# Memory values of the cross attention as three products of split parts, and what is moved for them

## What is computed

```python
def memory_cross_attention(h, mem_n, w_q, w_kv, w_o):
    b, s, _ = h.shape
    m = mem_n.shape[1]
    q = (h @ w_q).reshape(b, s, X_HEADS, X_HEAD_DIM) * (X_HEAD_DIM ** -0.5)
    kv = (mem_n @ w_kv).reshape(b, m, 2, X_HEADS, X_HEAD_DIM)
    k, v = kv[:, :, 0], kv[:, :, 1]
    sc = jnp.einsum('bshd,bmhd->bhsm', q, k, preferred_element_type=jnp.float32)
    p = jax.nn.softmax(sc, axis=-1).astype(v.dtype)
    o = jnp.einsum('bhsm,bmhd->bshd', p, v).reshape(b, s, D_MODEL)
    return o @ w_o
```

## Time and profile before

| | |
|---|---|
| Median of three runs | 2304.41 us (2298.34 to 2307.32) |
| The profiled execution | 2296.69 us, its span 2294.9 us |
| TensorE matmul busy | 2047.0 us, 89% of the span |
| VectorE busy | 847.7 us, 37% |
| ScalarE busy | 681.8 us, 30% |
| Chain that ended last | TensorE 66%, DMA 26%, VectorE 3% |
| Mean granted TensorE clock | 0.937 of full speed |

### The profile page before, as it was taken

The page is one execution under the profiler, slowest core; times in us unless marked ns, Lnnn a source line. Parts: engine busy times, 40 slices in busy tenths (PEclk is TensorE's granted clock), DMA queues, the critical chain, the costliest instruction groups (busy, mean ns, idle before and its releaser), DMA issues.

```text
span 2294.9 us, 38064 instructions
## 1 busy us (share of the span) xinstructions
PE 2047.0 (89%) x16924; PEld 1362.6 (59%) x16924; DVE 847.7 (37%) x1251; ACT 681.8 (30%) x995; POOL 40.6 (2%) x65
## 2 busy tenths in 40 slices
PE   8999987877779998987877789998999998989998
PEld 6877433333328876433333339565899895657996
DVE  6433211000006433111111127236677572365774
ACT  5433111111115433111111125214444352144443
POOL 1000000000001000000000000000000000000000
PEclk9999798888889999888888899999999999999999
DMA  8155899999996167899999996221754352116540
GB/s 318 55 187 235 328 429 428 428 429 429 428 422 238 38 220 298 330 428 428 428 429 429 428 410 215 77 69 44 231 184 166 122 206 77 57 56 221 184 174 19
DMA packets 139088, 592.28 MB, mean 258 GB/s; under 512 B 5681, under 2 KB 59137, under 8 KB 114385
## 3 DMA queue, kind: packets, MB, share of 16 engines
q1 hardware_dynamic: 137856, 586.67, 64.6%
q0 software_dynamic: 1104, 3.70, 0.4%
HBM read 589.30 MB, written 1.05 MB: 257 GB/s over the span
## 4 chain that ended last, share of the span: by engine, by line
PE 66%; DMA 26%; DVE 3%; issue 2%; ACT 1%; SPq 1%; DVEq 0%; POOLq 0%; ACTq 0%; POOL 0%
PE ps L570 30%; DMA ring<-in_w_up 24%; PE ps L1150 11%; PE ps L2115 5%; PE ps L886 2%; PE ps L1955 2%; PE ps L1041 2%; DMA ring<-in_w_in 1%; PE ps L2154 1%; PE ps L1117 1%; DVE ring_lo L546 1%; PE ps L587 1%; DMA ring<-in_xattn_w_q 1%; PE ps L985 1%; PE ps L1072 1%
## 5 line engine op out<-in xcount | busy, mean ns | idle before, releaser
L1150 PE MATMUL ps<-ring,area 128*32 128x512 f32 x1984 | 313.5, 716 | 137.4 <-DMA ring<-in_w_up 137.4
L546 DVE TENSOR_TENSOR ring_lo<-ring,slab_hi 128x2048 fp32r<-128x2048 f32 x128 | 293.0, 2292 | 226.1 <-ACT slab_hi L541 225.9
L541 ACT ACTIVATE slab_hi<-ring 128x2048 fp32r<-128x2048 f32 x128 | 244.4, 1913 | 273.3 <-PE ps L570 243.5
L1150 PEld LDWEIGHTS ps<-ring,area 128*32 128x32 f32 x1984 | 74.0, 128 | 340.2 <-DMA ring<-in_w_up 172.7
L570 PE MATMUL ps<-hT_hi,slab_hi 128*128 128x256 f32 x832 | 234.9, 282 | 5.0 <-DVE ring_lo L546 1.9
L570 PE MATMUL ps<-hT_lo,slab_hi 128*128 128x256 f32 x832 | 233.4, 280 | 0.0
L570 PE MATMUL ps<-hT_hi,ring_lo 128*128 128x256 f32 x832 | 232.6, 280 | 0.0
L1720 DVE TENSOR_TENSOR area<-ps,par 128x256 f32<-128x256 f32 x32 | 13.6, 424 | 500.3 <-PE ps L1117 500.3
L1378 ACT ACTIVATE area<-ps 128x512 f32<-128x512 f32 x32 | 19.1, 597 | 557.7 <-PE ps L1150 557.7
L1171 PE MATMUL ps<-ring,area 128*32 128x512 f32 x992 | 150.3, 759 | 33.3 <-DVE area L1740 29.8
L570 PEld LDWEIGHTS ps<-hT_hi,slab_hi 128*128 128x128 f32 x832 | 156.0, 188 | 6.5 <-DVE ring_lo L546 2.3
(11 more groups left out here) (365 smaller groups left out, 2933.6 us busy)
## 6 DMA issues: line engine op xcount, KB each, us to landing
ring<-in_w_up SPq DMA_DIRECT2D x64, 2048.0 KB, 20.3
ring<-in_w_down SPq DMA_DIRECT2D x62, 2048.0 KB, 22.1
ring<-in_w_gate SPq DMA_DIRECT2D x60, 2048.0 KB, 14.9
ring<-in_w_ffn_up SPq DMA_DIRECT2D x44, 1024.0 KB, 7.7
ring<-in_w_in SPq DMA_DIRECT2D x18, 2048.0 KB, 10.2
ring<-in_w_ffn_down SPq DMA_DIRECT2D x10, 2048.0 KB, 7.9
ring<-in_xattn_w_kv SPq DMA_DIRECT2D x8, 2048.0 KB, 19.2
ring<-in_w_in SPq DMA_DIRECT2D x10, 1024.0 KB, 13.2
```

Of the source, the lines that this page charges most:

```text
L541: return m.nc.scalar.activation(hi, whole, ACT.Copy)
L546: return m.nc.vector.tensor_tensor(lo, whole, hi, ALU.subtract)
L1150: ins = mm(ps[32 * g:32 * g + CAP, 1, :], m.tokT[:, k, :], gate_up[i][:, k % 4, (g % 2) * BANK:(g % 2 + 1) * BANK], start=k == 0, stop=k = ...
```

## The change

- `PLAN1` gets another slot order: slab 11 (second queries) goes to slot 0 where it was in slot 5, slab 12 (first values) to slot 5 where it was in slot 0; all others stay. Each slot still has three slabs.
- Four halves H_XV to H_XV+3 of split weights are added; the halves of the output move up by four. The memory is split too: `mem_hi` (ScalarE copies 128x2048 to the place of `xn`) and `mem_lo` (VectorE subtracts, in the place of `memT`). The values are made of `exact` products, by halves of the contraction.
- Since `mem_lo` takes the place of `memT`, VectorE adds the two parts again at the end of layer 0's attention (`mem_whole`), and ScalarE waits for that before it writes to `xn`. The waste of `norm_squares` goes to `xp` in the cross attention.
- On ScalarE the splits of H_XO and H_XO+1 go from right behind the queries to later: the first in front of the eviction of values 1, the second behind half the transposed probabilities. The splits of the values stand among the evictions of the queries, around the eviction of values 0. On VectorE the low parts of H_XV+2 and H_XV+3 come ahead of the maxima, those of H_XO and H_XO+1 behind L1647.

```diff
-PLAN1, LANDED1, HELD1 = ring_plan([(i % SLOTS, 1) for i in range(18)])
+PLAN1, LANDED1, HELD1 = ring_plan([(s, 1) for s in (0, 1, 2, 3, 4, 5, 0, 1, 2, 3, 4, 0, 5, 1, 2, 3, 4, 5)])
-H_IN, H_OUT, H_XQ, H_XO, HALVES1 = 0, 7, 11, 15, 19
+H_IN, H_OUT, H_XQ, H_XV, H_XO, HALVES1 = 0, 7, 11, 15, 19, 23
...
+    m.mem_hi, m.mem_lo = over("mem_hi", xn_at, 0, KD, T), over("mem_lo", area_at, 0, KD, T)
...
     def memory_values(j):
 
-        w = weights(W_XV + j)
-        for t in range(NT):
-            for k in range(KD):
-                ins = mm(ps[:, 2 * j + t, :], m.memT[:, k, t * P:(t + 1) * P], w[:, k, :], start=k == 0, stop=k == KD - 1)
-                if k == 0 and release:
-                    free_released(ins)
-            ins.then_inc(m.s(f"xv{j}_full"), 1)
+        if j == 0:
+            pe.wait_ge(*at("mem_hi", l))
+            pe.wait_ge(*at("mem_lo", l))
+        for half in range(2):
+            w = parts(H_XV + 2 * j + half, BANK)
+            for t in range(NT):
+                for k in range(4):
+                    kk = 4 * half + k
+                    start, ins = exact(m, ps[:, 2 * j + t, :], [a[:, kk, t * P:(t + 1) * P] for a in (m.mem_hi, m.mem_lo)],
+                                       [a[:, k, :] for a in w], kk == 0, kk == KD - 1)
+                    if release:
+                        free_released(start)
+                if half == 1:
+                    ins.then_inc(m.s(f"xv{j}_full"), 1)
+            if half == 0:
+                ins.then_inc(m.s("half_used"), 1)
         release.append(W_XV + j)
...
-    norm_squares(m, act, at("x_mixed", l), s("h2_sq"))
+    norm_squares(m, act, at("x_mixed", l), s("h2_sq"), m.xp.rearrange("p t h n -> p t (h n)"))
+    go(m.mem_hi[:, :, :], m.memT, ACT.Copy).then_inc(s("mem_hi"), 1)
     for b in range(4):
         if b < 2:
             split(H_XQ + 2 + b, "xq_full", b + 1)
         act.wait_ge(*at("xq_full", l, b + 1))
+        if b == 2:
+            split(H_XV, "xq_full", 3)
         go(m.xqT[:, 2 * b:2 * b + 2, :], two(ps[:, 4 + b, :]), ACT.Copy).then_inc(s("xq_cols"), 1)
-    split(H_XO, "xq_full")
-    split(H_XO + 1, "xq_full")
+    split(H_XV + 1, "xq_full")
...
+    split(H_XV + 2, "half_used", 5)
     memory_values(0)
+    split(H_XV + 3, "xv0_full")
     for t in range(NT):
         act.wait_ge(*at("xs_max", l, t + 1))
...
+    split(H_XO, "half_used", 6)
     memory_values(1)
     for b in range(2):
         act.wait_ge(*at("xpT_full", l, b + 1))
         go(m.xpT[:, 0, 2 * b:2 * b + 2, :], two(ps[:, 4 + b, :]), ACT.Copy).then_inc(s("xpT_a"), 1)
+    split(H_XO + 1, "xv1_full")
...
-    split(H_XO + 2, "half_used", 5)
+    split(H_XO + 2, "half_used", 7)
...
+    if l + 1 < L:
+        act.wait_ge(*at("mem_whole", l))
...
+    dve.wait_ge(*at("mem_hi", l))
+    dve.wait_ge(*at("xk_full", l))
+    v.tensor_tensor(m.mem_lo[:, :, :], m.memT, m.mem_hi[:, :, :], ALU.subtract).then_inc(s("mem_lo"), 1)
-    for q in range(H_XQ + 2, H_XO + 2):
+    for q in range(H_XQ + 2, H_XV + 4):
         split(q)
...
+    split(H_XO)
+    split(H_XO + 1)
     for b in range(4):
         dve.wait_ge(*at("xo_cols_a", l, b + 1))
...
+    if l + 1 < L:
+        dve.wait_ge(*at("xv1_full", l))
+        v.tensor_tensor(m.memT, m.mem_hi[:, :, :], m.mem_lo[:, :, :], ALU.add).then_inc(s("mem_whole"), 1)
     split(H_XO + 2)
```

More of the change, by code:

```diff
@@ L341 @@
 group("mla_pe", second=[("q2_full", 4), ("kv2_full", 4), ("qk2_T", 8), ("br2_full", 8), ("merged_T", 4), ("out3_half", 1), ("up_full", 2 * NUP), ("dn_half", NF // 2 - 1)])
-group("half_pe", first=[("half_used", 5)])
+group("half_pe", first=[("half_used", 7)])
+group("mem_hi", first=[("mem_hi", 1)])
+group("mem_lo", first=[("mem_lo", 1), ("mem_whole", 1)])
 group("parts_hi", first=[("w1_hi", HALVES1)], second=[("w2_hi", HALVES2), ("w_hi", 2 * NUP + NF // 2)])
@@ L400, in allocate @@
     m.x = sb("x", NT, D)
+    xn_at = -(-nc.sbuf_base // 32) * 32
     m.xn = sb("xn", NT, D)
@@ L815, in half1 @@
     first, i = ((W_IN1, q // 2) if q < H_OUT else (W_OUT1, q - H_OUT) if q < H_XQ else
-                (W_XQ, (q - H_XQ) // 2) if q < H_XO else (W_XO, q - H_XO))
+                (W_XQ, (q - H_XQ) // 2) if q < H_XV else (W_XV, (q - H_XV) // 2) if q < H_XO else (W_XO, q - H_XO))
     if first == W_IN1:
@@ L819, in half1 @@
     slot, size = PLAN1[first + i].slot, SLAB // 2
-    buffer = (q - max(h for h in (H_IN, H_OUT, H_XQ, H_XO) if h <= q)) % 2
+    buffer = (q - max(h for h in (H_IN, H_OUT, H_XQ, H_XV, H_XO) if h <= q)) % 2
     if first == W_XQ:
@@ L823, in half1 @@
         return first + i, m.hi[:, buffer].rearrange("p (k n) -> p k n", k=KD), cut(m.ring_lo), cut(m.ring)
-    at = IN_HALF[q] * size if first == W_IN1 else 0
+    at = IN_HALF[q] * size if first == W_IN1 else buffer * size if first == W_XV else 0
     return first + i, m.hi[:, buffer], m.ring_lo[:, slot, at:at + size], m.ring[:, slot, at:at + size]
@@ L1193, in tensor_experts, with norm_squares @@
     expert(E - 1, last=True)
-def norm_squares(m, act, x_ready, done):
+def norm_squares(m, act, x_ready, done, junk=None):
     sem, count = x_ready
@@ L1201, in norm_squares @@
         act.wait_ge(sem, count - (NT - 1 - t))
-        act_squares(m, act, [m.x[:, t, :]], [m.xn[:, t, :]], [m.stat[:, t:t + 1]], D ** -0.5, done)
+        act_squares(m, act, [m.x[:, t, :]], [(m.xn if junk is None else junk)[:, t, :]], [m.stat[:, t:t + 1]], D ** -0.5, done)
 def two(bank):
@@ L2487, in scalar_second @@
         split_in(2)
-        norm_squares(m, act, at("x_first", 0), s("n1_sq"))
+        norm_squares(m, act, at("x_first", 0), s("n1_sq"), m.xn)
     else:
@@ L2610, in scalar_second @@
     split(1)
-    norm_squares(m, act, at("h_mixed", l), s("n2_sq"))
+    norm_squares(m, act, at("h_mixed", l), s("n2_sq"), m.xn)
     for j in range(NUP):
```

## The result

The changed kernel took 2282.18 us (median of four runs, 2277.15 to 2283.18); the kernel before 2304.67 us over four runs. The ratio is 0.9904 with a 95% interval of 0.9882 to 0.9925: 22 us less, where 12.2 were forecast and 15 was the most that the range allowed. Two things stand beside each other. Against its own profiled execution (2296.69 us) the forecast was 2284.5, and the profiled execution of the changed kernel took 2283.18. Against the medians it was out of its range by 2 us.

A forecast was written before the change was run, and what follows sets the result against it. The chain was 66% TensorE and 26% DMA, with cross attention a row of TensorE pieces. Products 10.4 us plus slot order 1.8 us made 12.2 us off the 2304.4 us median: 2292.2 us, range 2284 to 2301 us.

The forecast's parts named there:

- Products: Cross-attention values: 48 matmuls of 11.14 us replace 13.73 us of plain float32 per slab, saving 10.4 us over four slabs.
- Slot order: Queries' second slab loads earlier, so TensorE's 0.9 us standstill between query halves goes in both layers: 1.8 us saved.
- Splits, moved work, new operations: Value splits, moved output splits and memory copies on ScalarE and VectorE cost nothing; tightest slack 0.8 us.
- Rival B: Value splits become the chain and TensorE waits at each half: 2327 us if fully in series, chance 0.05.
- rival C: New ring order does nothing, the queries' second slab stays late: 1.8 us not won, 2294 us, chance 0.07.
- The sum against the profiled execution: Whole kernel: the profiled execution of 2296.69 us less 12.2 us saved gives 2284.5 us.
- the one from there to the median: Whole kernel: the profiled execution was 7.7 us below the median, so 2304.4 - 12.2 = 2292.2 us, 0.53% less.
- the second block's length unchanged: Sign to look for: first block ends 12 us earlier while the second block keeps its length.
- Rival A: Experts' loads or the clock take the gain back, 2 to 4 us a layer either way: 2298 us, chance 0.18.

The follow-up runs named there:

- e4: Changed kernel with the old slot order put back: 2283.95 us, ratio 0.9913 to the kernel before.
- e3: Kernel before with the new slot order alone, values still plain float32: 2300.98 us, ratio 0.9981 to the kernel before.
- e16: Kernel before with seven extra unused matmuls a layer while TensorE waits in the choice of tokens: 2297.10 us, ratio 0.9967 to the kernel before.
- e6: Kernel before with 3 of 16 plain matmuls of each memory-value slab left out in both layers: 2284.68 us, ratio 0.9907 to the kernel before.
- e8: Kernel before with 3 of 16 plain matmuls of each value slab left out in layer 0 alone: 2295.44 us, ratio 0.9957.
- e9: Kernel before with 3 of 16 plain matmuls of each value slab left out in layer 1 alone: 2294.45 us, ratio 0.9960.
- e5: Changed kernel with a fourth product, low by low, in the memory values: 2302.44 us, ratio 0.9981 to the kernel before.
- e10: Kernel before with 1 of 16 plain matmuls of each value slab left out in both layers: 2299.65 us, ratio 0.9971.
- e11: Kernel before with 2 of 16 plain matmuls of each value slab left out in both layers: 2297.37 us, ratio 0.9969.

## Why the prediction was right and wrong

**Products: right.** 48 matmuls took 11.21 us where 11.14 were forecast, from the row of the attention's output. The rates of 216 and 131 ns that were weighed against it would have made 10.4 and 6.3 us: the measured 11.21 / 48 = 234 ns disagrees with both.

**Slot order: right in the chain, a little small.** The load is issued at 106.07 us, the four halves run without a gap, and e4 brings the standstill back. The standstill was read as 0.9 us from the start of a ScalarE row that itself comes after the end of the matmuls; e3 shows 1.2 (24.07 less 22.84 us). In the times e3 gives 4.4 us (1.2 to 7.8), which holds the 1.8.

**Splits, moved work, new operations: right.** All slacks held; the tightest was 0.9 us (0.8 forecast). Rival B is refuted by the one piece of 34.05 us, rival C by the load at 106.07.

**The sum against the profiled execution: right for the attentions, and close in the whole by luck** (2284.5 forecast, 2283.18 measured, spans 2294.9 and 2281.0). The 12.2 us are in the two attentions, as worked out. That the whole executions differ by 13.5 us is luck: the first profiled span of before was 6.1 us below the mean of its five, that of the changed kernel 2.5 below the mean of its four, and the means differ by 17.5.

**The step that failed** is the one from there to the median: "against the median: 2304.4 - 12.2 = 2292.2 us". It took the 7.7 us between the profiled execution and the median for a fixed amount that the change would carry along. It was none. The profiled execution of before was a short one of a kernel that scatters over 15 us; that of the changed kernel was its slowest of four. The term that the sum put at nothing is the one of the untouched stages ("the second block's length unchanged"): the runs show 20 to 22 us of saving, 8 to 10 more than the attentions give, and the traces show the second block 4.3 us shorter. The row that warned was in the table: a profiled execution below all three runs shown.

**Rival A had the place and not the size.** It gave 2 to 4 us a layer to the clock "in either direction", and the forecast counted the good direction in only as an upper bound of 15 us of saving. That the clock matters beyond the attention is shown by e16 and, within the kernel before, by the second block's rows. That it is what the change gained by is not shown: in the second block's first row the changed kernel is shorter at no higher clock. That loads take the gain back was not seen: the experts' rows differ by +0.6 and -0.3 us in the means, less than single traces of one kernel differ from each other (2 to 4 us in most).

**What stays open.** Shown: the extra 9 us come without the new kind of work as soon as the attention is 10 us shorter (e6), come in either layer (e8, e9), and are not proportional to the length (e5, e10, e11); e5 has 6.5 us of extra with a longer attention, so the length alone isn't it either. Seen in nine traces: the untouched rows of the second block are 4.3 us shorter in the mean, and 2.4 of them are waits that end just after code has landed. Argued and not shown: that a change of the attention or of the number of instructions shifts the stages behind it so that fewer of their waits come, or fewer bring a fall of the clock. Why before does so badly, and where the half of the 9 us lies that the traces don't hold, was not settled. An experiment that keeps TensorE busy in the second block's waits was not made, nor one that changes only the number of instructions.

## What to carry to other kernels

Cost an edit of matmul form by a row of the very form that it gets, its operands' roles included; the chain in order of time then gives the stage to 0.1 us. Before a sum of half a per cent is set against a median, look how the runs scatter and where the profiled execution stands among them: if it lies outside the runs, the untouched stages are not constant, and the range must be at least as wide as the scatter of before on the side of the gain. Where TensorE waits a few us for other engines and has real work behind it, throwaway matmuls in the wait can be worth more than they cost. In a stage of many small matmuls, look at the waits without a releaser too: an edit far ahead can move them.

## What the runs showed of the hardware

- One program's executions scattered over 15 us (2297.74 to 2312.55, 23 runs, standard deviation 3.8) and the changed kernel's over 3.6 (2283.27 to 2286.84, six runs, 1.5), on the same chip in turns; the mean granted clock of an execution went with its time (correlation -0.8 over the 23).
- Seven unused matmuls of 0.86 us a layer in TensorE's waits kept the granted clock of that stretch at 1.00 where it had been 0.89 to 0.93, and saved 6 us of 2303 by the medians, 8 by the ratio.
- Removing 3.4, 6.9 and 10.3 us of TensorE time from the same place saved 6.7, 7.1 and 21.5 us, each known to 3 to 5 us.
- In a stretch with 3539 matmuls in 212 us TensorE stood still two to five times, for 0.8 to 4.7 us, without a releaser in the profile. All 70 such waits of over 0.7 us in the second block's two long rows, in nine traces, ended 1.2 to 1.6 us after a DMA packet of kind "instruction" had landed.
